# The last half output group of a decoder layer, computed token set by token set, and warm-up matmuls in its first stage

## The chip, the cores and the metric

The kernel runs on one core of one Trainium2 chip. The metric is the device time of one execution in microseconds (us), the median of several runs.

## What is computed

One layer of a decoder over 320 tokens (256 prompt tokens, 8 samples of 8 tokens), width 4096. Attention, indexer and pooling branches end in a mixed activation of 4096 channels. Only this part of the reference bears on the change:

```
h = einsum('btd,dn->btn', rmsnorm(x, ln_g), w_in)       # input projection, 14496 columns
...
mix = concatenate([o_a * silu(g_a), o_b * silu(g_b)])
y = x + einsum('btm,md->btd', mix, w_out)                # w_out 4096 x 4096
rmsnorm(y, g) = y * rsqrt(mean(y*y, axis=-1) + 1e-6) * g # final norm, over all 4096 columns
```

## The kernel before, in words

**Products.** Activations stand in SBUF with channels on the partitions and tokens on the free axis, split into a high and a low part (`XH`, `XL`, type fp32r). Weights come in chunks of 512 rows by 256 columns (`raw`, four slots). ACT rounds a chunk to `hi` (`hi_chunk`, L238), DVE subtracts to get `lo` (`lo_chunk`, L242), and PE forms hi·XH, hi·XL and lo·XH with the weights stationary and all 320 tokens moving (`products`, L267 to L269): 24 matmuls of 320 columns to a chunk. In the segment `qi` a shorter form is used (`paired`, L254 and L255): 512 and 256 moving columns.

**Order.** A group is 512 output columns: two halves of 8 chunks each. Each engine runs its own program over the chunks j = 0..15 of a group (`pe_quad`, `act_quad`, `dve_quad`); extra work is woven in at fixed j. ACT and DVE split chunk j + 3 while PE is at chunk j; a split waits until the chunk four before has been used (`chunk_used`), since `hi` and `lo` have four slots. SP issues the loads, a chunk's load after the `lo` split of the chunk four before it.

**Last stage.** The segment `out` has 8 groups. After a half, DVE copies two banks of 128 channels x 320 tokens to `stg` (L372). PE turns a group's four blocks for the three sets of tokens (128, 128 and 64 tokens; `turn`, L1539, 12 transposes), DVE adds x (`residual`, L1525), ACT squares and sums (`squares`, L1469), POOL multiplies by `final_g` (`weigh`, L1627). For groups 0 to 6 this is woven into the next group. After group 7 nothing follows: copies, turn, residual, squares, the sum (L1669, L1671), the root (L1654), a Newton step (L1679 to L1687), the scaling of all 3 x 4096 columns by DVE (L1688) and ACT (L1655) in eight pieces, and their stores by SP (L1552) and ACT (L1458), 5.2 MB in all.

**First stage.** SP and ACT load the 320 rows of x in five column parts for each of the three sets (`x_part`, L452; parts 0 and 1 are 512 columns, 2 to 4 are 1024), small tensors, and the first chunks (`first_chunk`, 160 columns wide, 320 KB). PE waits for the small tensors, turns them (L595), then for each chunk c turns the next chunk's x (`turn_tokens`, L605: for each of 4 channel blocks two transposes of 128-row sets and one of the 64-row set) and runs `products(c)`. ACT rounds each block to XH (L513), splits weight chunks (L238) and squares x (L524), in that order for each c; DVE makes XL (L542) and `lo`. Chunks 8 and 9, whose splits belong to c = 6, are 256 columns wide.

Of the kernel before, what the change touches and what calls it, by code (L numbers as in the profile page):

```python
# [32 lines left out]
def hybrid_layer(nc, t, out):  # L33
# [90 lines left out]
    with root:  # L124
# [109 lines left out]
        def hi_chunk(act, c, slot, uses, width=2 * P, guard=True):  # L234
# [3 lines left out]
            nc.scalar.activation(hi[:, slot, :, 0:width], raw[:, slot, :, 0:width], ACT.Copy).then_inc(hi_ready, 1)  # L238

        def lo_chunk(dve, c, slot, width=2 * P):  # L240
            dve.wait_ge(hi_ready, c + 1)
            nc.vector.tensor_tensor(lo[:, slot, :, 0:width], raw[:, slot, :, 0:width],  # L242
                                    hi[:, slot, :, 0:width].bitcast(F32), ALU.subtract).then_inc(lo_ready, 1)
# [28 lines left out]
        def pe_quad(pe, name, q, weave=None, before=None, first=False, last=False):  # L272

            _, _, _, c0, quad0, _ = segs[name]
            for j in range(QC):
# [17 lines left out]
        def act_quad(act, name, q, weave=None, last=False, turned=None, gate=None, open_end=False):  # L293

            _, _, _, c0, quad0, tile0 = segs[name]
            for j in range(QC):
                k = j + AHEAD_SPLIT
                half = j // CH
                if not (last and k >= QC):
# [46 lines left out]
        def dve_quad(dve, name, q, weave=None, last=False, turned=None, gate=None, open_end=False, first=False):  # L346
# [3 lines left out]
            for j in range(QC):  # L350
                k = j + AHEAD_SPLIT
                if not (last and k >= QC):
                    lo_chunk(dve, q * QC + (c0 + k), (c0 + k) % SLOTS)
                if j in ends.values():
# [45 lines left out]
        s_onehot, s_wi = sem("s_onehot"), sem("s_wi")  # L400
# [23 lines left out]
        def first_stage(ph):  # L424
# [20 lines left out]
            junk = keep[:, G * N:G * N + XW]  # L445

# [7 lines left out]
            def on_sync(sp):  # L454
                def first_chunk(c):
                    load_chunk(sp, c, c % SLOTS, w_rows["w_in"][:, KK * c:KK * c + KK, C_WI:C_WI + W0], W0, c >= SLOTS)
                sp.dma_start(ident[:], t["c_ident"]).then_inc(s_small, 16)
                x_part(sp, 0, 0)
                sp.dma_start(gN[:], t["ln_g"][0].rearrange("(k p) -> k p", p=P)).then_inc(s_small, 16)
                sp.dma_start(pscN[:], t["pool_scale"][0].rearrange("(k p) -> k p", p=P)).then_inc(s_small, 16)  # L460
# [19 lines left out]
            def on_gpsimd(pool, ahead):  # L480
                pool.dma_start(ptab[:], t["page_table"].rearrange("(o b) p -> o (b p)", o=1)).then_inc(s_outA, 16)
# [20 lines left out]
            def on_scalar(act):  # L502
                for part in range(len(X_CUTS)):
                    x_part(act, 1, part)
                    if part < 3:
                        x_part(act, 2, part)
# [23 lines left out]
            def on_vector(dve):  # L530
                nc.vector.memset(ssq[:], 1.0).then_inc(s_step, 1)
# [61 lines left out]
            def on_tensor(pe):  # L593
                pe.wait_ge(s_small, 48)
# [4 lines left out]
                def turn_tokens(c):  # L599
                    for k in range(KK * c, KK * c + KK):  # L600
# [652 lines left out]
        def last_stage(ph):  # L1253
# [6 lines left out]
            assert DECK >= 3 * D + 8 * P  # L1260
# [21 lines left out]
            y = [deck[:, i * D:(i + 1) * D] for i in range(3)]  # L1282
            gq, sqj = (deck[:, 3 * D + 4 * P * i:3 * D + 4 * P * (i + 1)] for i in range(2))
            NQ_OUT = segs["out"][2]
            sq = sb("sq", [P, 3, NQ_OUT], ctx=ph)
            ms = sb("ms", [P, 3], ctx=ph)
            rt = sb("rt", [P, 3], ctx=ph)
            nt = sb("nt", [P, 3], ctx=ph)
            rf = sb("rf", [P, 3], ctx=ph)
# [89 lines left out]
            def dve_weave(dve, q, j):  # L1379
# [21 lines left out]
                if s == 6:  # L1401
# [6 lines left out]
            (f_mul, f_hi, f_lo, f_t, f_add, f_sq, f_gq, f_g, f_sum, f_rt, f_rf, f_x, f_gd) = (sem(n) for n in (  # L1408
                 "f_mul", "f_hi", "f_lo", "f_t", "f_add", "f_sq", "f_gq", "f_g", "f_sum", "f_rt", "f_rf", "f_x", "f_gd"))
            f_y = {e: sem(f"f_y_{e}") for e in ("act", "dve")}  # L1410
            f_out = {e: sem(f"f_out_{e}") for e in ("act", "dve")}
# [25 lines left out]
            def gate_branch(pool, m):  # L1437
# [8 lines left out]
            CUTS = {"dve": ((0, 0, D // 2), (0, D // 2, D), (2, 0, D // 2), (2, D // 2, D)),  # L1446
                    "act": ((1, 0, D // 4), (1, D // 4, D // 2), (1, D // 2, 3 * D // 4), (1, 3 * D // 4, D))}

            def scaled(eng, name, mul):
                eng.wait_ge(f_rf, 1)  # L1450
                eng.wait_ge(f_g, NQ_OUT)
                eng.wait_ge(f_gd, 1)
                for n, (i, a, z) in enumerate(CUTS[name]):
                    r = TT[i][1]
                    mul(y[i][0:r, a:z], rf[0:r, i:i + 1]).then_inc(f_y[name], 1)
                    if name != "dve":
                        eng.wait_ge(f_y[name], n + 1)
                        eng.dma_start(outs[i][:, a:z], y[i][0:r, a:z]).then_inc(f_out[name], 16)  # L1458
                if name != "dve":
                    eng.wait_ge(f_out[name], 16 * len(CUTS[name]))  # L1460

            def squares(act, q):

                for i in range(3):
# [5 lines left out]
                                         accum_out=sq[0:r, i, ds(q, 1)]).then_inc(f_sq, 1)  # L1470

# [54 lines left out]

            def dve_out_weave(dve, q, j):
                if j == 2:
                    residual(dve, q - 1)

# [16 lines left out]
            def on_sync(sp):  # L1547
                load_segment(sp, "ga")
                load_segment(sp, "out")
                for n, (i, a, z) in enumerate(CUTS["dve"]):  # L1550
                    sp.wait_ge(f_y["dve"], n + 1)
                    sp.dma_start(outs[i][:, a:z], y[i][0:TT[i][1], a:z]).then_inc(f_out["dve"], 16)  # L1552
                sp.wait_ge(f_out["dve"], 16 * len(CUTS["dve"]))

# [14 lines left out]
            def on_gpsimd(pool):  # L1569
# [48 lines left out]
                def weigh(q, tiles_):  # L1618
# [6 lines left out]
                    for i in tiles_:  # L1625
                        cols = y[i][0:TT[i][1], ds(q * (4 * P), 4 * P)]
                        ins = nc.gpsimd.tensor_tensor(cols, cols, gq[0:TT[i][1], :], ALU.mult)  # L1627
                    ins.then_inc(f_g, 1)

                with pool.Fori(0, NQ_OUT - 1) as q:  # L1630
# [3 lines left out]
                    weigh(q, (0, 1, 2))  # L1634
                weigh(NQ_OUT - 1, (0, ))
# [4 lines left out]
            def on_scalar(act):  # L1640
# [10 lines left out]
                act_quad(act, "out", NQ_OUT - 1, act_out_weave, True, turned=f_t)  # L1651
                squares(act, NQ_OUT - 1)
                act.wait_ge(f_sum, 3)
                nc.scalar.activation(rt[:], ms[:], ACT.Sqrt).then_inc(f_rt, 1)  # L1654
                scaled(act, "act", lambda o, r: nc.scalar.activation(o, o, ACT.Copy, scale=r))  # L1655

            def on_vector(dve):
# [8 lines left out]
                dve_quad(dve, "out", NQ_OUT - 1, dve_out_weave, True, turned=f_t)  # L1666
                residual(dve, NQ_OUT - 1)
                dve.wait_ge(f_sq, 3 * NQ_OUT)
                nc.vector.tensor_reduce(ms[:], sq[:], AX.X, ALU.add).then_inc(f_sum, 1)  # L1669
                dve.wait_ge(f_sum, 2)  # L1670
                nc.vector.tensor_scalar(ms[:], ms[:], 1.0 / D, EPS, ALU.mult, ALU.add).then_inc(f_sum, 1)  # L1671
                dve.wait_ge(f_gq, 16 * NQ_OUT)
                for i in (1, 2):
                    cols = y[i][0:TT[i][1], D - 4 * P:D]
                    ins = nc.vector.tensor_tensor(cols, cols, gq[0:TT[i][1], :], ALU.mult)
                ins.then_inc(f_gd, 1)

                dve.wait_ge(f_rt, 1)
                nc.vector.reciprocal(rt[:], rt[:]).then_inc(f_sum, 1)  # L1679
                dve.wait_ge(f_sum, 4)  # L1680
                nc.vector.tensor_tensor(nt[:], rt[:], rt[:], ALU.mult).then_inc(f_sum, 1)
                dve.wait_ge(f_sum, 5)
                nc.vector.tensor_tensor(nt[:], nt[:], ms[:], ALU.mult).then_inc(f_sum, 1)
                dve.wait_ge(f_sum, 6)
                nc.vector.tensor_scalar(nt[:], nt[:], -0.5, 1.5, ALU.mult, ALU.add).then_inc(f_sum, 1)
                dve.wait_ge(f_sum, 7)
# [117 lines left out]
```

## Time and profile before

| | us |
|---|---|
| median of three runs (2142.09 to 2143.4) | 2143.34 |
| the profiled execution | 2144.88 |
| its span, first to last instruction | 2143.4 |
| PE busy in the span | 2099.1 |

The span is what the instructions cover; 1.5 us lie around it. Engines: PE is the matmul engine, PEld its weight loads, DVE the vector engine, ACT the scalar engine, POOL the general engine; SP only issues transfers. A matmul's row shows its whole passage; matmuls overlap, so the distance between starts is what one costs. A name in square brackets after a row is what ended the idle time before it.

### The profile page before, as it was taken

What the parts mean: (1) busy time and instruction counts of PE and PEld (TensorE: products, weight loads), DVE (VectorE), ACT (ScalarE), POOL (GpSimd) and SP (SyncE); (2) the same over time, 40 slices, a digit from 0 to 9 for tenths busy, and PEclk for the clock granted to TensorE, in tenths of its full rate; (3) what the DMA queues carried; (4) which work ended last, traced back from release to release, by engine and by line L of the source; (5) the groups of instructions that cost most, each with busy time, mean ns of one, the idle gap of its engine ahead of it and who ended that gap; (6) DMA issues with size and microseconds to landing.
All of it is one profiled execution on the core that took longest, in us unless ns stands there. A gap on an engine that the chain in (4) does not pass through costs nothing.

```text
span 2143.4 us, 38938 instructions
## 1 busy us (share of the span) xinstructions
PE 2099.1 (98%) x14287; PEld 1996.1 (93%) x14287; DVE 1156.0 (54%) x1375; ACT 741.4 (35%) x911; POOL 404.1 (19%) x560
## 2 busy tenths in 40 slices
PE   7999999999999999999999999999999999999994
PEld 6888888899999999999999999999999999999994
DVE  4545454555555445656776667655656644444442
ACT  5433333332323333333332323333334333333332
POOL 0100000021211010235660102222223211111110
PEclk9999999999999999999999999999999999999998
DMA  6677777755554566566665657777777655555553
GB/s 191 188 222 212 215 213 207 226 155 154 157 154 138 175 186 174 174 197 182 201 184 175 186 166 212 241 233 224 228 229 258 216 165 163 161 160 162 163 152 108
DMA packets 339501, 402.38 MB, mean 188 GB/s; under 512 B 20173, under 2 KB 316301, under 8 KB 338793
## 3 DMA queue, kind: packets, MB, share of 16 engines
q1 hardware_dynamic: 293736, 294.53, 47.0%
q0 software_dynamic: 27952, 86.77, 12.7%
q10 hardware_dynamic: 17744, 20.19, 2.8%
q8 instruction: 41, 0.67, 0.1%
q14 instruction: 28, 0.22, 0.0%
HBM read 374.04 MB, written 31.51 MB: 189 GB/s over the span
## 4 chain that ended last, share of the span: by engine, by line
PE 93%; DMA 2%; POOL 2%; DVE 1%; ACT 1%; issue 0%; SPq 0%; ACTq 0%; POOLq 0%; DVEq 0%
PE bank L267 22%; PE bank L269 22%; PE bank L268 22%; PE bank L254 11%; PE bank L255 6%; PE wide L749 1%; PE wide L1314 1%; PE wide L1159 1%; PE wide L1344 1%; PE wide L1327 1%; POOL ubuf L1044 1%; PE wide L605 1%; PE wide L726 1%; DMA projT<-stg 1%; DMA xN<-x_prompt 1%; PE wide L1539 0%
## 5 line engine op out<-in xcount | busy, mean ns | idle before, releaser
L267 PE MATMUL bank<-XX,hi 128*128 128x320 f32 x3392 | 1072.7, 316 | 2.9 <-DVE XX L1484 2.9
L242 DVE TENSOR_TENSOR lo<-raw,hi 128x1024 fp32r<-128x1024 f32 (+1 forms) x552 | 700.9, 1274 | 667.4 <-ACT hi L238 666.8
L269 PE MATMUL bank<-XX,lo 128*128 128x320 f32 x3392 | 1051.2, 310 | 0.0
L268 PE MATMUL bank<-XX,hi 128*128 128x320 f32 x3392 | 1051.0, 310 | 0.0
L238 ACT ACTIVATE hi<-raw 128x1024 fp32r<-128x1024 f32 (+1 forms) x552 | 577.0, 1052 | 868.6 <-PE bank L269 547.0
L267 PEld LDWEIGHTS bank<-XX,hi 128*128 128x128 f32 x3392 | 639.3, 188 | 12.6 <-issue 5.0
L268 PEld LDWEIGHTS bank<-XX,hi 128*128 128x128 f32 x3392 | 639.5, 189 | 2.1
L269 PEld LDWEIGHTS bank<-XX,lo 128*128 128x128 f32 x3392 | 638.9, 188 | 0.0
L254 PE MATMUL bank<-XX,hi 128*128 128x512 f32 x1024 | 355.7, 392 | 0.0
L255 PE MATMUL bank<-XX,lo 128*128 128x256 f32 x1024 | 287.1, 280 | 0.0
L254 PEld LDWEIGHTS bank<-XX,hi 128*128 128x128 f32 x1024 | 191.6, 187 | 42.0 <-issue 0.2
L255 PEld LDWEIGHTS bank<-XX,lo 128*128 128x128 f32 x1024 | 193.9, 189 | 0.0
L1627 POOL TENSOR_TENSOR deck<-deck 128x512 f32 (+2 forms) x22 | 34.7, 1598 | 368.9 <-ACT deck L1469 368.9
L495 POOL DMA_DIRECT2D biasP<-biasD x16 | 8.7, 541 | 283.9 <-PE bank L255 283.9
L764 ACT ACTIVATE relu<-wide 128x384 f32<-128x384 f32 (+1 forms) x32 | 14.0, 437 | 120.0 <-PE wide L726 86.9
L370 DVE TENSOR_TENSOR stg<-bank,rstdB 128x320 f32<-128x320 f32 x72 | 32.0, 485 | 39.8 <-PE bank L269 39.8
L669 POOL DMA_DIRECT2D ipg<-cache_idx_k x64 | 34.6, 541 | 99.8 <-issue 99.8
L1559 POOL DMA_DIRECT2D deck<-cache_k x64 | 34.5, 540 | 97.1 <-issue 97.1
L1012 POOL DMA_DIRECT2D oT<-ohT x16 | 8.8, 549 | 176.9 <-ACT ohT L1187 176.9
L1227 DVE MAX8 tops<-scS 64x8 f32<-64x1032 f32 x32 | 39.1, 1221 | 0.0
L1044 POOL TENSOR_TENSOR ubuf<-ubuf 128x1816 f32<-128x1816 f32 (+3 forms) x10 | 38.8, 3879 | 0.8
L1559 POOL DMA_DIRECT2D keep<-cache_v x40 | 21.5, 537 | 91.2 <-issue 91.2
(244 smaller groups left out, 1309.3 us busy)
## 6 DMA issues: line engine op xcount, KB each, us to landing
raw<-w_in SPq DMA_DIRECT2D x416, 512.0 KB, 3.8
raw<-w_out SPq DMA_DIRECT2D x128, 512.0 KB, 3.7
deck<-cache_k POOLq DMA_DIRECT2D x64, 256.0 KB, 4.1
projT<-stg ACTq DMA_DIRECT2D x36, 320.0 KB, 2.9
keep<-cache_v POOLq DMA_DIRECT2D x40, 256.0 KB, 3.3
deck<-cache_v POOLq DMA_DIRECT2D x24, 256.0 KB, 3.8
ipg<-cache_idx_k POOLq DMA_DIRECT2D x64, 64.0 KB, 2.6
wp<-w_pool POOLq DMA_DIRECT2D x4, 1024.0 KB, 6.0
```

The costliest lines, as they stand in the source:

```text
L238: nc.scalar.activation(hi[:, slot, :, 0:width], raw[:, slot, :, 0:width], ACT.Copy).then_inc(hi_ready, 1)
L242: nc.vector.tensor_tensor(lo[:, slot, :, 0:width], raw[:, slot, :, 0:width], hi[:, slot, :, 0:width].bitcast(F32), ALU.subtract).then_inc( ...
L254: nc.tensor.matmul(both, wh, XX[:, k, :, FREE:N], start=first, stop=False)
L255: mm = nc.tensor.matmul(bank[banks[n]][:, LATE:2 * LATE], wl, XX[:, k, 0, FREE:N], start=False, stop=last)
L267: nc.tensor.matmul(sums, wh, XH[:, k, :], start=first, stop=False)
L268: nc.tensor.matmul(sums, wh, XL[:, k, :], start=False, stop=False)
L269: mm = nc.tensor.matmul(sums, wl, XH[:, k, :], start=False, stop=last)
L669: pool.dma_start(ipg[:, p, :], tile_rows(t["cache_idx_k"][0], page)).then_inc(s_ipg, 16)
L1044: done(nc.gpsimd.tensor_tensor(dst[:, :, lost + w:UW], src[:, :, lost + w:UW], src[:, :, lost:UW - w], ALU.add))
L1227: nc.vector.max(tops[:], scS[:]).then_inc(ts_step, 1)
L1559: pool.dma_start(dst[p], tile_rows(src, page)).then_inc(landed, 16)
L1627: ins = nc.gpsimd.tensor_tensor(cols, cols, gq[0:TT[i][1], :], ALU.mult)
```

## The change

The last group's second half is computed with the tokens stationary and 256 weight columns moving. Its first half is turned and added on its own, after chunk 1 of the second half. Chunks 0 and 1 are multiplied for all three sets; then chunks 2 to 7 for set 0, then for set 1, then for set 2. Chunks 6 and 7 get buffers of their own (`late`), so that no weight is overwritten. After each set's products: residual, squares, root, Newton step, scaling in seven pieces and six stores for this set alone. The last 256 columns of `final_g` are multiplied in by DVE with the scaling. The output rows move to buffers that outlive the stage (`ends`, and `keep` for set 2).

In the first stage PE starts with 16 bf16 matmuls of 512 columns on zeros. SP's order of loads changes, x parts 3 and 4 go to POOL's queue behind the landing of part 0, and `turn_tokens` turns the eight 128-row blocks first and then the four 64-row blocks.

```diff
+            def set_products(pe, i, m):
+                c0, r = TT[i]
+                for kk in range(KK):
+                    k = (KK * m + kk + KT // 2) % KT
+                    wh, wl = (w[:, kk, :] for w in weights[m])
+                    sums = bank[SETS[i]][0:r, 0:HB]
+                    nc.tensor.matmul(sums, XH[:, k, c0:c0 + r], wh, start=m == 0 and kk == 0, stop=False)
+                    nc.tensor.matmul(sums, XL[:, k, c0:c0 + r], wh, start=False, stop=False)
+                    mm = nc.tensor.matmul(sums, XH[:, k, c0:c0 + r], wl, start=False, stop=m == CH - 1 and kk == KK - 1)
+                return mm
+            def pe_last_half(pe):
+                pe.wait_ge(evac[1], Z + (quad0 + 1))
+                for m in range(CH):
+                    pe.wait_ge(lo_ready, c + 1)
+                    for i in range(3 if m < NOW else 1):
...
+                        mm = set_products(pe, i, m)
+                    mm.then_inc(chunk_used if m < CH - 1 else f_prod, 1)
+                    if m == 1:
+                        last_turn(pe)
+                for i in (1, 2):
+                    for m in range(NOW, CH):
+                        mm = set_products(pe, i, m)
+                    mm.then_inc(f_prod, 1)
+            def act_end_weave(act, q, j):
+                act_out_weave(act, q, j)
+                if j == 10:
+                    for i in range(3):
+                        half_square(act, i, 0, 3 * Z + i)
+                if j == 12:
+                    nc.scalar.activation(rt[:], sq[:, :, 0], ACT.Sqrt).then_inc(f_rt, 1)
...
             def on_scalar(act):
...
+                act.wait_ge(f_g, NQ_OUT)
+                for i in range(3):
+                    half_square(act, i, 1, 3 * NQ_OUT + i)
+                    last_root(act, i)
+                    act_scaled(act, i)
...
             def on_vector(dve):
...
+                for i in range(3):
+                    dve.wait_ge(f_prod, i + 1)
+                    last_residual(dve, 1, i)
+                    last_norm(dve, i)
+                    dve_scaled(dve, i)
...
             def on_sync(sp):
+                sp.dma_start(gN[:], ...)
+                sp.dma_start(pscN[:], ...)
                 sp.dma_start(ident[:], t["c_ident"]).then_inc(s_small, 16)
                 x_part(sp, 0, 0)
-                sp.dma_start(gN[:], ...)
-                sp.dma_start(pscN[:], ...)
+                x_part(sp, 0, 1)
                 first_chunk(0)
-                x_part(sp, 0, 1)
                 x_part(sp, 0, 2)
-                first_chunk(1)
-                first_chunk(2)
-                x_part(sp, 0, 3)
-                x_part(sp, 2, 3)
-                first_chunk(3)
-                x_part(sp, 0, 4)
-                x_part(sp, 2, 4)
+                for c in range(1, SLOTS):
+                    first_chunk(c)
...
             def on_gpsimd(pool, ahead):
+                pool.wait_ge(s_x[0], 48)
+                for part in (3, 4):
+                    for i in range(3):
+                        x_part(pool, i, part)
...
             def on_tensor(pe):
+                pe.wait_ge(s_zeros, 1)
+                for _ in range(WARM):
+                    nc.tensor.matmul(bank[1][:, 0:512], zeros[:, 0:P], zeros, start=True, stop=True)
                 pe.wait_ge(s_small, 48)
...
-                        for i, (c0, r) in enumerate(TT):
-                            tr = nc.tensor.transpose(sbank[k % 4][:, c0:c0 + r], xN[i][0:r, k * P:k * P + P],
-                                                     ident[0:r, 0:r])
-                        tr.then_inc(s_xT, 1)
+                        for i, (c0, r) in enumerate(TT[0:2]):
+                            nc.tensor.transpose(sbank[k % 4][:, c0:c0 + r], xN[i][0:r, k * P:k * P + P], ident[0:r, 0:r])
+                    for k in range(KK * c, KK * c + KK):
+                        nc.tensor.transpose(sbank[k % 4][:, T_P:N], xN[2][0:N_S, k * P:k * P + P],
+                                            ident[0:N_S, 0:N_S]).then_inc(s_xT, 1)
```

## Rows read from the trace of the kernel before

**Rows 1.** The page of the profile: busy time by engine, and the chain by engine.

```profile
PE 2099.1 (98%) x14287; PEld 1996.1 (93%) x14287; DVE 1156.0 (54%) x1375; ACT 741.4 (35%) x911; POOL 404.1 (19%) x560
...
PE 93%; DMA 2%; POOL 2%; DVE 1%; ACT 1%; issue 0%; SPq 0%; ACTq 0%; POOLq 0%; DVEq 0%
```

**Rows 2.** The view of waits, for PE: who waited for whom, us in total, times, longest.

```profile
PE bank L595 <- DMA pscN<-pool_scale: 7.7, 1, 7.7
```

**Rows 3.** The timeline of the end: start us, us, engine, line, operation, tiles, shapes.

```profile
2115.05 0.89 DVE L372 COPY stg<-bank 128x320 f32<-128x320 f32 x2 [11.70 <-PE bank L269]
...
2116.03 1.50 PE L1539 MATMUL wide<-ident,stg 128*128 128x128 f32 x12 [1.03 <-issue]
2117.64 1.88 DVE L1525 TENSOR_TENSOR deck<-wide,deck 128x512 f32<-128x512 f32 x3 [1.71 <-PE wide L1539]
2118.42 0.63 ACT L1469 ACTIVATE deck<-deck 128x512 f32<-128x512 f32 x1 [16.33 <-DVE deck L1525]
2118.95 0.19 ACT L1469 ACTIVATION_READ_ACCUMULATOR deck<-deck 128x1 f32 x1
...
2123.37 0.16 DVE L1679 RECIPROCAL rt<-rt 128x3 f32<-128x3 f32 x1
...
2124.16 0.16 DVE L1687 TENSOR_TENSOR rf<-rt,nt 128x3 f32<-128x3 f32 x1
2124.36 1.15 ACT L1655 ACTIVATE deck<-deck,rf 128x1024 f32<-128x1024 f32 x1 [1.86 <-DVE rf L1687]
2124.36 4.87 DVE L1688 TENSOR_SCALAR deck<-deck,rf 128x2048 f32<-128x2048 f32 x4
...
2130.31 0.35 ACTq L1458 DMA_DIRECT2D out<-deck  x1
```

**Rows 4.** The DMA view from 2100 us to the end: rate in 40 equal slices.

```profile
GB/s 0 0 0 0 0 0 0 0 0 0 0 0 0 0 0 15 0 0 0 0 0 0 0 0 417 391 458 402 402 421 369 253 242 250 264 253 238 376 30 0
```

**Rows 5.** Windows of the end, PE alone: window, us, PE busy, granted clock, DMA share, GB/s.

```profile
2120.00:2124.00 4.00, 0.00 (x0) 0.86 0.00 0
```

**Rows 6.** The timeline around 68 us, PE: matmuls that move 256 and 512 columns.

```profile
68.10 0.28 PE L255 MATMUL bank<-XX,lo 128*128 128x256 f32 x1
68.10 0.19 PEld L254 LDWEIGHTS bank<-XX,hi 128*128 128x128 f32 x1
68.22 0.40 PE L254 MATMUL bank<-XX,hi 128*128 128x512 f32 x1
...
68.45 0.28 PE L255 MATMUL bank<-XX,lo 128*128 128x256 f32 x1
```

**Rows 7.** The timeline of the last half group: one split on ACT, one on DVE.

```profile
2093.99 1.06 ACT L238 ACTIVATE hi<-raw 128x1024 fp32r<-128x1024 f32 x1 [2.46 <-PE bank L269]
...
2098.60 1.23 DVE L242 TENSOR_TENSOR lo<-raw,hi 128x1024 fp32r<-128x1024 f32 x1 [2.29 <-ACT hi L238]
```

**Rows 8.** The timeline of the first stage, PE and ACT.

```profile
14.16 0.74 ACT L238 ACTIVATE hi<-raw 128x640 fp32r<-128x640 f32 x1 [1.88 <-DMA raw<-w_in]
...
16.09 3.73 PE L605 MATMUL wide<-ident,xN 128*128 128x128 f32 x12 [4.37 <-DMA xN<-x_prompt]
...
19.75 0.63 PE L267 MATMUL bank<-XX,hi 128*128 128x320 f32 x1
...
25.13 2.30 PE L605 MATMUL wide<-ident,xN 128*128 128x128 f32 x12
...
42.07 1.06 ACT L524 ACTIVATE keep<-xN 128x1024 f32<-128x1024 f32 x1
...
43.27 2.24 ACT L513 ACTIVATE XX<-wide,gT 128x320 fp32r<-128x320 f32 x4
...
60.37 0.42 PE L267 MATMUL bank<-XX,hi 128*128 128x320 f32 x1
```

**Rows 9.** The DMA view of the first stage, issues from 3.1 to 3.4 us: KB, us to landing.

```profile
raw<-w_in SPq DMA_DIRECT2D x1, 320.0 KB, 11.2
xN<-x_prompt SPq DMA_DIRECT2D x1, 256.0 KB, 12.7
```

More of the change, by code:

```diff
@@ L270, in products, with pe_quad @@
             mm.then_inc(chunk_used, 1)
-        def pe_quad(pe, name, q, weave=None, before=None, first=False, last=False):
+        def pe_quad(pe, name, q, weave=None, before=None, first=False, last=False, stop=QC):
             _, _, _, c0, quad0, _ = segs[name]
-            for j in range(QC):
+            for j in range(stop):
                 half, pos, rot = chunk_at(name, j, first, last)
@@ L344, in act_segment, with dve_quad @@
                 act_quad(act, name, q, weave, gate=gate)
-        def dve_quad(dve, name, q, weave=None, last=False, turned=None, gate=None, open_end=False, first=False):
+        def dve_quad(dve, name, q, weave=None, last=False, turned=None, gate=None, open_end=False, first=False, homes=None):
             _, _, _, c0, quad0, _ = segs[name]
@@ L351, in dve_quad @@
                 k = j + AHEAD_SPLIT
-                if not (last and k >= QC):
+                if homes and k in homes:
+                    lo_chunk(dve, q * QC + (c0 + k), k % SLOTS, homes=homes[k])
+                elif not (last and k >= QC):
                     lo_chunk(dve, q * QC + (c0 + k), (c0 + k) % SLOTS)
-                if j in ends.values():
+                if j in ends.values() and not (homes and j == QC - 1):
                     half = chunk_at(name, j, first)[0]
@@ L502, in on_scalar @@
             def on_scalar(act):
-                for part in range(len(X_CUTS)):
+                for part in range(3):
                     x_part(act, 1, part)
-                    if part < 3:
-                        x_part(act, 2, part)
+                    x_part(act, 2, part)
                 act.wait_ge(s_step, 1)
@@ L1443, in gate_branch @@
                 ins.then_inc(f_mul, 1)
[L1446 to L1460, printed above, removed]
+            Z = NQ_OUT - 1
@@ new lines, in last_stage @@
+            HB = 2 * P
+            Z = NQ_OUT - 1
+            HB = 2 * P
+            homes = {QC - 2 + n: (late[:, 2 * n, :, :], late[:, 2 * n + 1, :, :]) for n in range(2)}
+            weights = [homes.get(CH + m, (hi[:, m % SLOTS, :, :], lo[:, m % SLOTS, :, :])) for m in range(CH)]
+            NOW = 2
+            assert segs["out"][3] % SLOTS == 0 and CH == 2 * SLOTS
+            SETS = (2, 3, 0)
+            CUTS = {"dve": ((0, D // 8), (D - HB, D), (D // 8, 5 * D // 16), (5 * D // 16, D // 2)),
+                    "act": ((D // 2, 5 * D // 8), (5 * D // 8, 13 * D // 16), (13 * D // 16, D - HB))}
@@ L1525, in residual, with last_residual, last_turn @@
                     nc.vector.tensor_tensor(cols, sbank[i][0:r, :], cols, ALU.add).then_inc(f_add, 1)
+            def last_residual(dve, half, i):
+                r = TT[i][1]
+                cols = y[i][0:r, half_cols(half)]
+                turned = bank[SETS[i]][0:r, 0:HB] if half else sbank[i][0:r, 0:HB]
+                nc.vector.tensor_tensor(cols, turned, cols, ALU.add).then_inc(f_add, 1)
+            def last_turn(pe):
+                pe.wait_ge(evac[0], segs["out"][4] + Z + 1)
+                pe.wait_ge(f_add, 3 * Z)
+                for i, (c0, r) in enumerate(TT):
+                    for n in range(2):
+                        tr = nc.tensor.transpose(sbank[i][0:r, n * P:(n + 1) * P], stg[0][:, n, c0:c0 + r], ident[:])
+                tr.then_inc(f_t, 1)
             def dve_out_weave(dve, q, j):
@@ L1650, in on_scalar @@
                     act_quad(act, "out", q, act_out_weave, turned=f_t)
[L1651 to L1655, printed above, removed]
+                act_quad(act, "out", Z, act_end_weave, True, turned=f_t, homes=homes)
+                act.wait_ge(f_g, NQ_OUT)
+                for i in range(3):
+                    half_square(act, i, 1, 3 * NQ_OUT + i)
+                    last_root(act, i)
+                    act_scaled(act, i)
             def on_vector(dve):
@@ L1711, in hybrid_layer @@
             prompt = prompt_stage(place)
-        last = last_stage(root)
+        last = last_stage()
         stages = (first, index, topk, prompt, last)
```

169 lines of the change are left out of this document (115 added, 54 removed).

## Prediction, made before the changed kernel was run

> **What bounds the kernel now.** I read the page first. PE is busy 98% of the span and carries 93% of the chain that ended last [rows 1]. So an edit pays only where PE idles or where its work shortens. PE idles in two places of any size: at the start, until the small tensors have landed at 7.7 us [rows 2] and again 4.37 us for x at 16.09 [rows 8]; and at the end, where the last product is through at 2115.0 and the span runs to 2143.4. The change works on exactly these two places.
>
> **The end before** [rows 3]. From 2115.0 on one step follows another: two copies 0.89, twelve transposes 1.50, three residual adds 1.88, three squares (0.63 + 0.19 each), the root, reciprocal and Newton steps to 2124.3, scaling to 2130.3, and the stores. The stores are the largest part: data moves from 2126.4, first at about 400, then at about 250 GB/s [rows 4], to the end. That is 28.4 us behind PE.
>
> **Part 1, the products of the last half.** A chunk on PE takes 2.46 + 1.06 = 3.52 us, the distance between two splits that each wait for PE [rows 7]; with 24 matmuls that is 0.1467 us for 320 columns, 0.458 ns a column. The last half (8 chunks, 192 matmuls) therefore costs 28.2 us and starts at 2086.8. The new form has 3 sets x 32 blocks x 3 = 288 matmuls of 256 columns. A 256-column matmul starts at 68.10, the next at 68.22, and 768 columns take 0.35 us from 68.10 to 68.45 [rows 6]: 0.46 ns a column again, with a 128-column weight load inside each. I take 256 x 0.458 = 0.1173 us: 288 of them are 33.8 us, **5.6 us more** on PE. Set 2 has half the tokens and pays the same, since the weights move. The page "TensorE: Matmul & The Clock Gate" of the Trainium skill, in "Back-to-back issue gap", gives columns / 2.4 + 2.5 ns; that would be 109 ns for 256 columns and 2.4 us less in all, but it also gives 136 ns for 320 columns, where the trace has 147, so the trace decides.
>
> **Inside the last half.** Chunks 0 and 1 take 36 matmuls each, 8.4 us, to 2095.2. Six transposes of the first half, at half of 1.50 us, reach 2096.0. Chunk 4 of the half is split once chunk 0 has been used, and is in time. The split of chunk 5 waits for chunk 1 (2095.2): ACT to 2096.3, DVE to 2097.6. Then DVE adds the first half for three sets, 0.38 each (a 512-column add takes 0.63, a 320-column copy 0.45 [rows 3]), and ACT squares them, about 0.63 each, to 2099.9. Only behind these squares in ACT's queue stand the splits of chunks 6 and 7 (1.06 each on ACT, 1.23 on DVE [rows 7]): ready at 2102.3 and 2103.5. PE takes 12 matmuls, 1.41 us, for a chunk of set 0 and would want chunk 6 at 2101.6. So it stalls about 0.7 us, and set 0 is through at 2105.1. Loads don't matter: the last one is issued under the split of chunk 3, near 2089, while PE wants it after 2102. POOL's last multiply waits for the squares and ends near 2102.5. The square-root table is fetched behind the last split, under set 0's products. Sets 1 and 2 need 72 matmuls each: 2113.5 and **2122.0**.
>
> **Each set's tail.** From the last product: residual 0.15 + 0.38, square and sum 0.7, root 0.25, reciprocal and three steps at 0.20 each [rows 3], so about 2.4 us to the scale factor. ACT's three pieces (1792 columns at 1.15 per 1024, plus three issues of 0.35 to 0.4 and gaps) take 3.4 us; DVE's take 1.8 and run beside. Set 0: last store issued at 2111. Set 1: at 2119.4. Its 2.1 MB at 250 GB/s, the slower rate of [rows 4], would be through at 2125 even from 2116.5. Set 2: scale factor at 2124.4, last store issued at 2127.6. It moves only 1.05 MB, 4.2 us at 250 GB/s from 2125.7. Both ways lead to 2130 to 2130.5. The span ends at 2130.5 instead of 2143.4: **12.9 us less**. What hides the cost of sets 0 and 1 is set 2's own products, 8.4 us a set against a tail of 5.8 us of engines and 8.4 us of stores at the slower rate.
>
> Bounds: at 0.109 a matmul, the distance of the transposes, (1.50 - 0.3) / 11 [rows 3], the gain is 15.3; if the two sets' stores drag into the third's, or splits stall PE 3 us more, 9.9.
>
> **Part 2, the first stage.** Before, products(0) starts at 19.75 [rows 8]. x part 1 of set 0 lands at 3.4 + 12.7 = 16.1, behind chunk 0 of the weights (2.9 + 11.2 = 14.1) in SP's queue [rows 9]. The change puts it ahead, so PE turns chunk 1's x near 10 us. Then products(0) waits for chunk 0. That transfer now has 256 KB more ahead of it on SP and POOL's 2.5 MB beside it from about 8 us, and 1 MB less on ACT's queue beside it. It can land at 12 to 17; I take 13.5, near the 14.1 of before. Rounding 0.74, DVE's subtraction 0.83 and gaps make it ready at 15.2: 4.5 us earlier than before.
>
> The warm-up matmuls aim at the clock. The trace shows half rate at the start: 12 transposes at 16.09 take 3.73, at 25.13 they take 2.30; products(0) takes 5.38 us from 19.75 to 25.13 where a chunk normally takes 3.52. So the lower level costs 1.9 us there (1.2 against 2.4 GHz). But after the warm-ups PE has only transposes until 15.2, with pauses for loads. At the end of the old trace the granted clock averages 0.86 over 2120 to 2124 although nothing ran there after 2117.5 [rows 5]: it falls a few microseconds after PE stops. I take it as lost again, and products(0) as slow as before, to 20.6. The Trainium skill's page "TensorE: Matmul & The Clock Gate", "Part 1: The HAM clock gate", says the same: the half rate is the default, and idling brings it back.
>
> From there ACT sets the pace, not PE. PE's cycle shortens: the 64-row transposes stand in one run instead of four, and twelve transposes with one change of shape should take about 1.4 in place of 2.13 us (2.30 with the overlap [rows 8]; twelve without such changes take 1.50 with it [rows 3]). A cycle would be 4.9 instead of 5.7. But ACT's work for a chunk is 2.24 for XH, 0.74 or 1.36 for splits and 2 x 1.25 for squares (1.06, and 0.19 for the sum as in [rows 3]) [rows 8]: 5.5, 5.5, 6.1, 6.1 and, with the two wide splits, 6.9 us for c = 2 to 6, together 30.0. With x of chunk 2 turned from 20.6 on, ACT starts on it at 21.4 and on chunk 7 at 51.4; DVE follows to 53.9; products(7) ends at 57.4. Before it started at 60.37 and ended 63.9 [rows 8]. **6.5 us less.** PE is the bound behind it, so the shift is carried to the end. Bounds: chunk 0 at 17 gives 3; at 12, with the clock kept, 9. Below that, loads held up further by POOL's queue could take all of it.
>
> What else moves: POOL's six issues stand before its page-table load, whose first user is far later; the wait for part 0 holds nothing else. ACT issues two transfers fewer. The memset for the warm-ups puts 0.3 us before DVE's others, hidden by the 7 us of loads. Longer straight-line code for PE I cost at nothing: the fetch runs beside the matmuls, and group 0 is straight-line too. If fetching failed, PE would pay it fully.
>
> **Sum.** 12.9 + 6.5 = 19.4 us. The profiled execution took 2144.88, of which 1.5 lie around the span: 2125.5. The median stands 1.5 below that execution: **2123.9**. A measurement tells about 0.2% (4.3 us) from no change.
>
> **Rivals.**
> *The first stage keeps its length* (chance 0.20). Speaking for it: three queues now draw on the same DMA engines, 320 KB took 11.2 us there with two, and ACT is nearly full. Against: what PE waited for at 16.09 was one transfer's place in a queue. Gain 1.5 there: 2143.3 - 12.9 - 1.5 = 2128.9.
> *The end gives less* (0.10). ACT and DVE serve the splits, squares and tails in one order each; each late split stalls PE. With 4 us lost: 2127.9.
> *Stationary loads are exposed* (0.03), the slower side. If a load of tokens were not hidden under 256 moving columns, a matmul would cost 0.117 + 0.109 = 0.226 (the load priced as a transpose, which has one of the same size under it), and the 288 would be 65.1 us: 31.3 more, 2155.2. It decides from (19.4 / 288) + 0.117 = 0.185 us a matmul. Against it stand [rows 6], a load under each of two neighbouring matmuls. For it: there the short ones come only every second time.
> *The warm-ups hold the clock* (0.15, inside the forecast): 1 us less, since ACT then binds: 2122.9.
>
> **How the numbers follow.** My forecast holds 0.67 with the last rival in it: 2120 to 2127.5. The range goes to the other two faster cases and the bounds: 2118 to 2131. Slower by over 0.2% is the exposed load, 0.03; within 0.2% needs both parts to fail by 15 us together, 0.03; faster 0.94.
>
> **What would show it.** Starts of the new matmuls 0.117 apart; the last one near 2115.5 on the new clock (2122.0 less 6.5); three stores of PE-covered sets; 8.4 us from PE's last product to the end; products(0) starting near 15 at 0.27 a matmul; products(7) starting near 53.9 behind DVE. I am wrong if the matmuls stand over 0.13 apart, if PE waits for splits over 2 us, or if products(7) starts after 58.

## The result, and the profile after

The changed kernel takes **2126.2 us** (2123.5 to 2127.8, four runs) against 2142.7 (2140.6 to 2143.4, four runs) of the kernel before, run beside it: ratio 0.9922, 95% interval 0.9910 to 0.9934, 16.5 us less. The forecast was 2123.9, within 2118 to 2131, and 19.4 us less. The profiled execution took 2127.56, its span is 2126.0, 17.4 us less than before. The page, as [rows 1]; the span's chain is followed back only to the last set's root here, so it has nothing to compare:

```profile
PE 2101.1 (99%) x14385; PEld 2001.3 (94%) x14393; DVE 1157.3 (54%) x1393; ACT 743.1 (35%) x925; POOL 406.7 (19%) x568
```

To see where the gain lies I cut every span at two instants: where DVE sums the squares of the first stage (L547 before, L554 after), and where DVE makes the last two copies of 128x320 (L372, L378), with which the last half begins.

| | first stage, to the sum of squares | middle | end, from the last copies |
|---|---|---|---|
| before | 62.66 | 2024.2 | 56.5 |
| after | 58.03 | 2022.1 | 45.8 |
| difference | -4.6 | -2.1 | -10.7 |

The first cut lies behind ACT and DVE. What is passed on to the middle is PE's part, the start of products(7): 60.37 before [rows 8], 56.63 now, 3.7 us earlier. Counted from there the middle is 3.0 us shorter, though the change does not touch it.

**The end.** The three sets on DVE, each from its residual add, and the last set's steps (the timeline of the changed kernel, DVE):

```profile
2099.35 0.43 DVE L1598 TENSOR_TENSOR ends<-bank,ends 128x256 f32<-128x256 f32 x1 [1.58 <-PE bank L1641]
...
2107.81 0.42 DVE L1598 TENSOR_TENSOR ends<-bank,ends 128x256 f32<-128x256 f32 x1 [4.17 <-PE bank L1641]
...
2116.05 0.42 DVE L1598 TENSOR_TENSOR keep<-bank,keep 64x256 f32<-64x256 f32 x1 [4.02 <-PE bank L1641]
...
2117.42 0.16 DVE L1530 RECIPROCAL rt<-rt 128x1 f32<-128x1 f32 x1 [0.16 <-ACT rt L1520]
...
2118.13 0.16 DVE L1537 TENSOR_TENSOR rf<-rt,nt 128x1 f32<-128x1 f32 x1
2118.32 0.48 DVE L1482 TENSOR_SCALAR keep<-keep,rf 64x512 f32<-64x512 f32 x1
```

The same on ACT, set 2:

```profile
2116.50 0.42 ACT L1513 ACTIVATE ends<-keep 64x256 f32<-64x256 f32 x1 [3.18 <-DVE keep L1598]
...
2118.32 0.72 ACT L1489 ACTIVATE keep<-keep,rf 64x512 f32<-64x512 f32 x1 [0.94 <-DVE rf L1537]
...
2121.95 0.49 ACTq L1494 DMA_DIRECT2D out<-keep  x1
```

The adds stand 8.46 and 8.24 us apart: one set's products each. The last one starts at 2116.05; its scale factor is ready 2.3 us later, ACT's last store is issued at 2121.95, and the span ends at 2126.0, 9.95 us behind the last add. PE's last product ends at 2116.0, so the span runs on for 10.0 us behind PE, where it was 28.4. Now PE, in the same timeline:

```profile
2096.20 0.28 PE L1641 MATMUL bank<-late,XX 128*128 128x256 f32 x1
2096.32 0.28 PE L1639 MATMUL bank<-late,XX 128*128 128x256 f32 x1
2096.44 0.28 PE L1640 MATMUL bank<-late,XX 128*128 128x256 f32 x1
...
2115.73 0.28 PE L1641 MATMUL bank<-late,XX 128*64 128x256 f32 x1
```

A 256-column matmul with a fresh 128-column load costs 0.12 us, start to start; on set 2, whose load has 64 columns, it costs 0.115. The DMA view in two windows, from 2109 to 2117.5 and from 2117.5 to 2126 (40 slices of 0.21 us each):

```profile
GB/s 0 0 0 0 0 0 0 0 0 0 0 164 366 424 337 405 376 424 376 419 376 376 419 390 376 419 405 376 376 419 376 376 420 419 419 361 275 0 0 0
```

```profile
GB/s 0 0 0 0 0 0 0 0 0 0 0 0 241 183 183 260 183 202 241 202 231 231 217 217 202 159 188 188 217 231 231 232 217 202 159 116 0 0 0 0
...
out<-keep SPq DMA_DIRECT2D x2, 192.0 KB, 3.2
out<-keep ACTq DMA_DIRECT2D x2, 192.0 KB, 3.8
```

Set 1's 2.1 MB move at 380 to 420 GB/s, under set 2's products. Set 2's 1.05 MB move at 210 (four pieces of 192 KB and two of 128) and take 5.0 us, from 2120.05 to 2125.1.

**The first stage.** ACT's rows (chunk 0, chunk 1, XH of chunk 2, XH of chunk 7), then PE's:

```profile
15.32 0.74 ACT L239 ACTIVATE hi<-raw 128x640 fp32r<-128x640 f32 x1 [1.76 <-DMA raw<-w_in]
...
23.84 0.74 ACT L239 ACTIVATE hi<-raw 128x640 fp32r<-128x640 f32 x1 [6.12 <-DMA raw<-w_in]
...
25.53 1.76 ACT L519 ACTIVATE XX<-wide,gT 128x320 fp32r<-128x320 f32 x4
...
54.10 1.76 ACT L519 ACTIVATE XX<-wide,gT 128x320 fp32r<-128x320 f32 x4
```

```profile
1.48 5.98 PE L603 MATMUL bank<-keep 128*128 128x512 bf16 x16 [1.48 <-DVE keep L537]
...
17.06 0.60 PE L268 MATMUL bank<-XX,hi 128*128 128x320 f32 x1 [1.30 <-DVE lo L244]
17.46 0.47 PE L269 MATMUL bank<-XX,hi 128*128 128x320 f32 x1
...
21.95 1.04 PE L615 MATMUL wide<-ident,xN 128*128 128x128 f32 x8
22.91 0.46 PE L617 MATMUL wide<-ident,xN 64*128 64x64 f32 x4
25.59 0.38 PE L268 MATMUL bank<-XX,hi 128*128 128x320 f32 x1 [2.21 <-DVE lo L244]
...
27.40 0.47 PE L269 MATMUL bank<-XX,hi 128*128 128x320 f32 x1
27.66 0.47 PE L270 MATMUL bank<-XX,lo 128*128 128x320 f32 x1
...
30.71 1.04 PE L615 MATMUL wide<-ident,xN 128*128 128x128 f32 x8
...
35.68 1.03 PE L615 MATMUL wide<-ident,xN 128*128 128x128 f32 x8
...
56.63 0.41 PE L268 MATMUL bank<-XX,hi 128*128 128x320 f32 x1 [0.92 <-DVE XX L549]
```

The warm-ups run from 1.48 to 7.4. Chunk 0 is split at 15.32, products(0) start at 17.06, 2.7 us earlier than in [rows 8], and at 0.27 us each until 19.9. Then comes a wait that did not exist before: chunk 1 is split only at 23.84, when it has landed, so products(1) start at 25.59; and from 26.9 to 30.1 the matmuls stand 0.27 apart once more. From 30.71 to 50.58 PE's five turns start 4.97 us apart, and PE does not wait until it is held up for 0.92 us before products(7). The granted clock of these stretches (windows of PE alone, the number behind the count in brackets):

```profile
2.00:7.00 5.00, 5.00 (x15) 1.00 0.77 226
7.00:12.00 5.00, 3.15 (x17) 0.77 1.05 252
12.00:17.00 5.00, 2.65 (x12) 0.50 1.06 309
17.00:22.00 5.00, 4.94 (x25) 0.71 1.05 338
22.00:27.00 5.00, 2.79 (x22) 0.98 1.09 259
27.00:32.00 5.00, 5.00 (x29) 0.68 0.66 174
```

It is 0.50 (1.2 GHz) from 12 to 17, and goes down twice: before the first products, and again after the pause for chunk 1 (0.68 on average from 27 to 32). The 1.00 from 2 to 7 can't be taken at its word: the 16 warm-ups last 5.98 us, where matmuls of the same kind cost about 0.215 us each at full rate (six in 1.47, four in 1.04, in e6 below), so most of them ran at the lower level. The column also reads 1.00 in the kernel before while its first products stand 0.27 apart [rows 8]. Before its first change the distance between starts is the measure, not this column. PE's waits of the changed kernel:

```profile
PE bank L268 <- DVE lo L244: 3.5, 2, 2.2
PE wide L1177 <- DMA uin<-projT: 2.5, 1, 2.5
PE wide L615 <- DMA xN<-x_prompt: 1.8, 1, 1.8
...
PE bank L1639 <- DVE late L244: 0.8, 1, 0.8
```

### The profile page after: what moved, and what is told of

Read it like the earlier page. It is cut to its first block and busy times, and to the rows that moved or that the text cites. A ratio compares the mean times of both kernels' runs of the same rounds, so it can differ in the third digit from the quotient of the medians.

```text
span 2126.0 us, 39179 instructions
## 1 busy us (share of the span) xinstructions
PE 2101.1 (99%) x14385; PEld 2001.3 (94%) x14393; DVE 1157.3 (54%) x1393; ACT 743.1 (35%) x925; POOL 406.7 (19%) x568
## 5 line engine op out<-in xcount | busy, mean ns | idle before, releaser
L268 PE MATMUL bank<-XX,hi 128*128 128x320 f32 x3328 | 1051.7, 316 | 5.8 <-DVE lo L244 3.5
L270 PE MATMUL bank<-XX,lo 128*128 128x320 f32 x3328 | 1030.3, 310 | 0.0
L269 PE MATMUL bank<-XX,hi 128*128 128x320 f32 x3328 | 1030.0, 309 | 0.0
L268 PEld LDWEIGHTS bank<-XX,hi 128*128 128x128 f32 x3328 | 626.9, 188 | 15.6 <-issue 8.8
L269 PEld LDWEIGHTS bank<-XX,hi 128*128 128x128 f32 x3328 | 627.0, 188 | 2.1
L270 PEld LDWEIGHTS bank<-XX,lo 128*128 128x128 f32 x3328 | 626.5, 188 | 0.0
L255 PEld LDWEIGHTS bank<-XX,hi 128*128 128x128 f32 x1024 | 191.5, 187 | 42.3 <-issue 0.2
L256 PEld LDWEIGHTS bank<-XX,lo 128*128 128x128 f32 x1024 | 193.5, 189 | 0.0
L1761 POOL TENSOR_TENSOR ends<-ends 128x512 f32 (+1 forms) x16 | 26.1, 1650 | 346.1 <-ACT ends L1503 328.7
L1240 DVE MATCH_REPLACE8 scS<-tops,scS 64x1032 f32<-64x1032 f32 x32 | 38.6, 1208 | 0.0
```

The lines of the kernel that those rows point to most:

```text
L255: nc.tensor.matmul(both, wh, XX[:, k, :, FREE:N], start=first, stop=False)
L256: mm = nc.tensor.matmul(bank[banks[n]][:, LATE:2 * LATE], wl, XX[:, k, 0, FREE:N], start=False, stop=last)
L268: nc.tensor.matmul(sums, wh, XH[:, k, :], start=first, stop=False)
L269: nc.tensor.matmul(sums, wh, XL[:, k, :], start=False, stop=False)
L270: mm = nc.tensor.matmul(sums, wl, XH[:, k, :], start=False, stop=last)
L1240: nc.vector.match_replace(scS[:], tops[:], scS[:], TAKEN).then_inc(ts_step, 1)
```

## The experiments

Times are medians with the kernel before run beside each; the columns "first stage", "middle" and "end" are cut from each run's profile at the instants above.

| kernel | median us | ratio to before (95%) | first stage | middle | end |
|---|---|---|---|---|---|
| changed kernel | 2126.2 | 0.9922 (0.9910 to 0.9934) | 58.03 | 2022.1 | 45.8 |
| e1 head only | 2136.1 | 0.9968 (0.9956 to 0.9979) | 55.74 | 2022.7 | 56.5 |
| e2 tail only | 2130.8 | 0.9933 (0.9920 to 0.9946) | 62.64 | 2022.0 | 45.95 |
| e3 no warm-ups | 2126.7 | 0.9920 (0.9907 to 0.9933) | 55.76 | 2023.6 | 45.9 |
| e4 old turn | 2128.6 | 0.9927 (0.9915 to 0.9939) | 60.16 | 2018.3 | 45.9 |
| e5 x later | 2124.7 | 0.9913 (0.9898 to 0.9928) | 53.58 | 2023.4 | 45.85 |
| e6 x later, clock held | 2121.9 | 0.9898 (0.9883 to 0.9913) | 52.31 | 2021.6 | 46.0 |
| e7 together | 2133.2 | 0.9953 (0.9937 to 0.9969) | 55.24 | 2020.1 | 55.8 |
| e8 rebalanced | 2123.3 | 0.9914 (0.9897 to 0.9931) | 54.30 | 2020.1 | 45.9 |
| e9 three chunks for all | 2122.9 | 0.9908 (0.9891 to 0.9924) | 55.80 | 2020.7 | 44.55 |
| e10 e6 + e9 | 2122.3 | 0.9902 (0.9885 to 0.9918) | 52.61 | 2025.7 | 44.6 |
| e11 e10 + part 2 later | 2120.3 | 0.9892 (0.9875 to 0.9908) | 51.96 | 2024.1 | 44.6 |
| e12 long rows (one run) | 2129.95 | | 55.24 | 2025.8 | 47.3 |

The end repeats within 0.15 us over the six kernels that share its code (the changed one and e2 to e6), the middle varies by 7.6 us in code that none of these edits touches. So an edit of the end is read from its column, not from the median; the first stage needs several profiles.

**e1 and e2, one half of the change each.** e1 is the kernel before with the new first stage, e2 the changed kernel with the old one.

> The kernel before with the new first stage alone, its end unchanged. Theory (two separate gains that add): the last half group starts 6.7 us earlier, as in the changed kernel (2080.1 against 2086.8), and the median is 6.7 us below that of the kernel before (ratio 0.9969). Rival (the first stage keeps its length and the whole gain is from the end): within 2 us of the kernel before. The first products start near 17.1 us at 0.27 us each.

> The changed kernel with the first stage of before. Theory: the end alone gives 10.7 us (the stretch from the start of the last half to the end of the span is 45.9 us instead of 56.6), ratio 0.995. Rival (the earlier end needs the new first stage, or part of the gain is common to both): under 8 us.

Measured: e1 has 6.9 us less in the first stage and an unchanged end, ratio 0.9968; e2 has an unchanged first stage and 10.6 us less at the end, ratio 0.9933. The two gains are separate and add up: by the cuts 6.9 + 10.6 = 17.5 us, where the span of the changed kernel is 17.4 shorter; by the medians 0.9968 x 0.9933 = 0.9901, a little below the changed kernel's interval. (e2's median is 13.6 us below the kernel before, 3 more than its end gives; its profile has the middle 2.2 us shorter.) The rival that the first stage keeps its length falls.

**e3, no warm-ups.**

```diff
-            WARM = 16
+            WARM = 0
```

> The changed kernel without its 16 warm-up matmuls. Theory (the clock falls back before the first products, so they buy nothing): time of the changed kernel within 0.7 us, first products again at 0.27 us each for the first 3 us or so. Rival (they shorten the stretch at half rate): 1 to 3 us slower than the changed kernel, more than 11 products at 0.27.

The first products start at 16.60, 0.5 us earlier, at the lower clock again; the medians are 0.5 us apart, and each interval is over 5 us wide, so a gain of 1 us would not show in them. The distance of 0.27 lasts longer than expected: it stands 20 times in products(0), against 9 in the changed kernel's profile. That is the rival's sign, but the warm-ups don't explain it: five more profiles with the same warm-ups and the same loads (e1, e7, e8, e9, e12) have it 20, 16, 4, 14 and 15 times. Their first stages are 54.3 to 55.8 us long, e3's is 55.76. So the warm-ups buy between nothing and 1.5 us where they stand, and these runs can't tell which.

**e4, the old order of the transposes,** in the changed kernel.

```diff
-                        for i, (c0, r) in enumerate(TT[0:2]):
+                        for i, (c0, r) in enumerate(TT):
...
-                    for k in range(KK * c, KK * c + KK):
-                        nc.tensor.transpose(sbank[k % 4][:, T_P:N], ...
```

> The changed kernel with the transposes of the first stage in their old order (three sets for each block). Theory (PE's turn takes 2.13 instead of 1.4 us and ACT gets the blocks one by one): cycles of 5.8 us instead of 5.0 for chunks 2 to 6, the last half starts 2.5 to 4 us later than in the changed kernel. Rival (ACT sets the pace anyway): under 1 us later, with ACT without idle time between 30 and 54 us.

The first stage ends at 60.16, against 54.3 to 55.8 in the six experiments with the new order and the same loads (e1, e3, e7, e8, e9, e12; 58.03 in the changed kernel's own profile). So the new order of the transposes is worth 4 to 6 us against these (2.1 against the changed kernel's own profile, which lost time at chunk 1), more than half of the first stage's gain. PE's rows show it free of that scatter: in e4 PE turns from 22.62 on every 5.84 us and never waits, in the changed kernel every 4.97, as expected (5.8 and 5.0): 0.87 us for each chunk. In ACT's rows of e4 XH of a chunk takes 2.24 us where ACT follows the turn block by block, and 1.77 for the last chunk, whose blocks had all been turned before ACT came; in the changed kernel every chunk from the second on takes about 1.76:

```profile
34.93 2.24 ACT L519 ACTIVATE XX<-wide,gT 128x320 fp32r<-128x320 f32 x4 [0.67 <-PE wide L615]
...
55.35 1.77 ACT L519 ACTIVATE XX<-wide,gT 128x320 fp32r<-128x320 f32 x4
```

The rival, that ACT sets the pace anyway, falls.

The median of e4 is 2.4 us above the changed kernel's, but the ratios overlap: this profile has the shortest middle of all (2018.3), and that hides the loss in its span (its last half starts 1.75 us earlier than the changed kernel's, not 2.5 to 4 later as expected).

**e5 and e6, what feeds the first products.**

```diff
-                pool.wait_ge(s_x[0], 48)
+                pool.wait_ge(s_x[2], 48)
```

> The changed kernel, but POOL issues x parts 3 and 4 when part 2 has landed (near 17 us) and not when part 0 has (9.5 us). Theory (POOL's 2.5 MB beside SP's queue make chunk 0 land at 15.3 and chunk 1 at 23.8): chunk 0 lands 1 to 2 us and chunk 1 3 to 5 us earlier, PE no longer waits 2.2 us for the split of chunk 1, 2 to 3 us faster than the changed kernel. Rival (the queue of SP alone, with its short rows, sets these landings): no change, and x parts 3 or 4 may come late, near 30 us or later.

Chunk 1 is split at 17.17 instead of 23.84, chunk 0 at 14.49 instead of 15.32; PE's wait for splits falls from 3.5 to 0.4 us, and PE now waits longer for x:

```profile
PE wide L615 <- DMA xN<-x_prompt: 4.3, 2, 2.2
...
PE bank L268 <- DVE lo L244: 0.4, 1, 0.4
```

The first stage ends at 53.58, about 2 us earlier than in e1, e3, e9. The theory holds for chunk 1: in the eight profiles with POOL's early issue it is split at 21.1 to 23.8, in the four with the later one (e5, e6, e10, e11) at 16.4 to 17.3. So POOL's 2.5 MB had been in its way. For chunk 0 it is not shown: without the edit it is split at 14.3 to 15.3, and 14.49 lies among these. The median is 1.5 us below the changed kernel's where 2 to 3 were expected, and the intervals overlap. e6 adds three groups of matmuls on zeros:

```diff
+                fill(6)
                 turn_tokens(0)
+                fill(4)
...
+                    if c == 0:
+                        fill(6)
```

> As the run before it, with 6, 4 and 6 more matmuls on zeros: behind the first 16, between the first two turns, and ahead of the first products. Theory (the clock is kept only by work close to the products): the first products stand 0.147 apart from the start, 1.3 to 1.9 us less for chunk 0; the added matmuls cost up to 1.5 us where loads were already in, so 0 to 1.5 us faster than the run before it. Rival (the clock falls anyway because the transposes in between do not keep it): first products at 0.27, 0 to 2 us slower.

The last fill runs until 15.6; the first products stand 0.147 apart from the second on (timeline of e6, PE):

```profile
14.15 1.47 PE L604 MATMUL bank<-keep 128*128 128x512 bf16 x6
16.43 0.39 PE L268 MATMUL bank<-XX,hi 128*128 128x320 f32 x1 [0.82 <-DVE lo L244]
16.66 0.31 PE L269 MATMUL bank<-XX,hi 128*128 128x320 f32 x1
16.81 0.31 PE L270 MATMUL bank<-XX,lo 128*128 128x320 f32 x1
```

Products(0) take 3.6 us instead of 5.1, and the first stage ends 1.3 us earlier than in e5 (one profile each; the ratios overlap). So the clock can be held: with fills in all three pauses, the last ending 0.8 us before the first product, no product stands 0.27 apart, while in every profile with warm-ups at the start alone some do. Which of the three fills is needed was not tried.

**e7, the three sets together.** All chunks for all sets, then three tails in a row; the same 288 matmuls.

```diff
-            NOW = 2
+            NOW = CH
...
-                for i in (1, 2):
-                    for m in range(NOW, CH):
-                        mm = set_products(pe, i, m)
-                    mm.then_inc(f_prod, 1)
```

> The changed kernel, but all three sets take every chunk, so that all sets end together and none of their adds, roots, scalings and stores lies under products. The same 288 matmuls. Theory (what pays is the stagger): PE ends up to 0.8 us earlier (no wait for the splits), then three tails of 5.9 us in a row and stores behind: 12 us slower than the changed kernel, near the kernel before. Rival (the shorter pieces and the first half done early are what pays): under 5 us slower.

The end is 55.8 us: 10 us longer than with the stagger (12 expected) and 0.7 shorter than before; the median is 7.0 us above the changed kernel's. The rival, under 5 us, falls. So what is left of the change without the stagger (smaller pieces, the first half finished early) just pays for the 5.6 us of extra products; the stagger is the gain. The stores then begin late and all stand behind PE (DMA view, 2100 to 2131):

```profile
GB/s 0 0 0 0 0 0 0 0 0 0 0 0 0 0 0 0 0 114 391 394 389 400 389 404 284 378 407 381 396 408 389 289 122 211 211 226 202 194 186 0
```

**e8, DVE scales 2560 columns of a set, ACT 1536 in two pieces.**

```diff
-            CUTS = {"dve": (..., (5 * D // 16, D // 2)),
-                    "act": ((D // 2, 5 * D // 8), (5 * D // 8, 13 * D // 16), (13 * D // 16, D - HB))}
+            CUTS = {"dve": (..., (5 * D // 16, 9 * D // 16)),
+                    "act": ((9 * D // 16, 3 * D // 4), (3 * D // 4, D - HB))}
```

> The changed kernel with DVE scaling 2560 columns of each set and ACT 1536 in two pieces (before: 2304 and 1792 in three). Theory (ACT's queue, 0.72 + 0.94 + 0.72 us of scaling and three issues, ends last): the last store is issued 1.1 us earlier and the span ends about 1 us earlier. Rival (the stores of 64 rows at 210 GB/s end last, whoever issues them): under 0.4 us.

```profile
2110.73 0.42 ACT L1513 ACTIVATE ends<-keep 64x256 f32<-64x256 f32 x1 [4.11 <-DVE keep L1598]
...
2115.09 0.50 ACTq L1494 DMA_DIRECT2D out<-keep  x1
```

From the square to ACT's last issue it is now 4.4 us where it was 5.45 (2116.50 to 2121.95), and the end is 45.9: nothing gained. The rival was right: the stores of 64 rows end last, not the engine that issues them (their data moves from about 2114.3 to 2119.4, at 210 GB/s again). Its lower median comes from a short first stage and middle.

**e9, three chunks for all sets.**

```diff
-            NOW = 2
+            NOW = 3
```

> The changed kernel with three chunks, not two, multiplied for all sets before set 0 runs ahead. Theory (PE waits 0.85 us for the splits of chunks 6 and 7, which one more chunk of 4.2 us covers; a stagger of 7.0 us still covers a tail of 5.9): the stretch from the last copies to the end of the span falls from 45.9 by 0.8 to 1.1 us. Rival (the shorter stagger lets the stores or tails of two sets meet): not shorter than 45.7.

The end is 44.55, 1.3 us less, a little more than the 0.85 that PE waited for the first of the two late splits; in the changed kernel there was a second, shorter hitch between the last two chunks of set 0 (0.26 us between two starts at 2097.5). In e9 PE does not wait for a split in the last half.

**e10 and e11, the gains put together.** e10 joins e6 and e9. e11 lets ACT issue x part 2 when part 0 has landed.

> x parts 3 and 4 later, the clock held up to the first products, and three chunks for all sets. Theory (the gains of e6 and e9 add): first stage as in e6 (its sum over squares near 52.3 us), last stretch as in e9, a median 1 us below that of e6, 5 us below the changed kernel.

> As e10, and ACT issues its two transfers of x part 2 when part 0 has landed. Theory (what is not needed yet takes the DMA engines from chunk 0 and x part 1): chunk 0 lands 1 to 2 us earlier, first products near 15, the first stage ends 0 to 1.5 us earlier than in e10. Rival (part 2 then becomes what the second chunk waits for, or the engines were not full): no gain, PE waits for x before its third turn.

First stage and end are as expected (52.6 and 44.6), but e10's median is 0.4 us above that of e6, where 1 below was expected: its profile has a middle of 2025.7, 4.1 us longer than that of e6. e11's first products start at 15.97 instead of 16.73 and its first stage ends 0.65 us earlier than e10's. At 2120.3 us, ratio 0.9892, e11 has the lowest median of all; against e6 and e10 the intervals overlap, against the changed kernel they don't.

**e12, long rows.** Set 2 stored in two transfers of 512 KB.

> The changed kernel, but set 2 is stored in two transfers of rows of 8 KB when all its columns of a half are scaled, not in six of 1 to 3 KB. Theory (64 rows are slow by their number, not their length: 250 GB/s with 8 KB rows before, 210 now): rate 210 to 250, the stores start 2 us later, last stretch 0.5 to 2 us longer. Rival (short rows cost the rate): 350 GB/s or more and a last stretch no longer than 45.9.

```profile
GB/s 367 426 377 426 386 198 0 0 0 0 0 0 0 0 0 0 0 0 0 0 211 211 291 132 291 132 185 238 79 344 79 344 79 344 26 396 0 0 0 0
...
out<-keep SPq DMA_DIRECT2D x1, 512.0 KB, 4.3
out<-keep ACTq DMA_DIRECT2D x1, 512.0 KB, 6.3
```

Set 2 moves in 4.9 us, 214 GB/s, and the end is 1.5 us longer. Rows of 8 KB are no faster than rows of 1 to 3 KB; and set 1, stored in the same pieces by the same two queues but with 128 rows, moved at 380 to 420. So the rate of these stores goes with the 64 rows, not with the length of a row.

## Why the prediction was right, and where it was off

- **PE idles only at the two ends.** Right: e1 and e2 separate them and they add up.
- **The matmul of 256 columns, 0.1173 us.** Right: 0.12 start to start, a set of 72 takes 8.24 to 8.46 (8.44 forecast). The rival of exposed loads is gone. The 109 ns by the Trainium skill's page "TensorE: Matmul & The Clock Gate", "Back-to-back issue gap", would have made a set 7.9.
- **The stall of 0.7 us at chunk 6.** Right in place and size: 0.85. It was the term that e9 removed. DVE's two late splits took 3.38 us together instead of 2 x 1.23. Why is open: POOL multiplied beside them, but by its rows only until 2096.4, and the second split was as slow as the first; the splits also write to another buffer, and no run parts the two:

```profile
2080.16 0.89 DVE L378 COPY stg<-bank 128x320 f32<-128x320 f32 x2 [1.14 <-PE bank L270]
...
2094.10 3.38 DVE L244 TENSOR_TENSOR late<-raw,late 128x1024 fp32r<-128x1024 f32 x2 [2.08 <-ACT late L239]
```

- **"Through at 2122.0", 35.2 us after the last half begins.** Measured 35.85, 0.65 more. The stall and the second hitch are 0.3 of it; the rest was not taken apart.
- **"Both ways lead to 2130 to 2130.5", 8.5 us behind PE: this step failed.** It was 10.0. The mechanism, stores of the last set, was right, its size was not: I took 250 GB/s from a mixed stretch of [rows 4], and 64-row stores run at 210, which is 5.0 us instead of 4.2; data starts about 0.35 us later than forecast, and 0.9 us pass from the last slice with data to the end of the span. I also held ACT's chain and the stores to be equal bounds; e8 shows that only the stores bind. Together: 12.9 us forecast, 10.7 measured.
- **Products(0) at 15.2.** Late by 1.9: chunk 0 was split at 15.32, inside the range of 12 to 17 but not at the 13.5 taken.
- **The clock.** Right that the warm-ups would be lost before the first products: the granted clock is 0.50 from 12 to 17 us. The Trainium skill's page "TensorE: Matmul & The Clock Gate", "Part 1: The HAM clock gate", says that idling brings the half rate back; the trace agrees. It also came back a second time, once PE had waited 2.2 us for chunk 1. Of the profiles with the early issue only this one shows the second fall; in the others PE waited 1.4 us or less there.
- **"From there ACT sets the pace, not PE": this step failed.** Forecast were 30.0 us of ACT's work from XH of chunk 2 to XH of chunk 7. Measured are 28.6, and 2.75 of them are waits for PE (1.75, 0.74 and 0.26 before three of its rows), so ACT's own work was 25.8: XH takes 1.76 instead of 2.24 when all blocks are there. PE set the pace, with its turns 4.97 us apart (4.9 forecast for its cycle); ACT and DVE held it up only before products(7), for 0.92 us. On the other side I missed chunk 1, at 23.8, and the second fall of the clock: XH of chunk 2 starts at 25.5, not 21.4. So products(7) start at 56.63 instead of 53.9, 3.7 us earlier than before instead of 6.5. In e1, e7, e8, e9 and e12, with the same first stage, they start at 52.9 to 54.4, which is 6.0 to 7.5 us earlier: there the number is met, but by PE's cycle and not by ACT's.
- **"PE is the bound behind it, so the shift is carried to the end".** Not shown: the middle varies by more than the shift. In the profiled pair it gave 3.0 us, counted from products(7), that were not forecast. Without this luck the two parts, 3.7 and 10.7, would have made 14.4 of the forecast 19.4.

## What to carry to other kernels

A last normalisation that needs whole rows holds the stores behind all products. Making the tokens stationary for the last slice, even with 20% more PE time in it, lets the scaling and storing of two sets of three go under products, provided that a set's products last longer than a set's tail; the size of the last set's store is what remains. Warm-up matmuls far ahead of the first real product showed no gain here, fills in the pauses up to it shortened the first stage by 1.3 us in one profile; before adding any, one should ask which load the first product waits for. In a kernel whose middle scatters by several us, cut the profile at fixed instants and judge an edit of an end by its own stretch.

## What had not been expected

The middle is 2018.3 to 2025.8 us long in fourteen profiles. In nine of them PE waits there for one load, `uin<-projT`: 0.9 us in e4 (the shortest middle), 1.9 in e6, 2.5 before and after, 5.2 in e12 (the longest), and in e10

```profile
PE wide L1183 <- DMA uin<-projT: 4.9, 1, 4.9
```

In the other five (e2, e3, e7, e8, e9) PE waits at about that place for DVE instead (`lg`), 1.8 to 2.5 us. Added to PE's waits for DVE's XX further on in the middle (1.4 to 3.3 us) this makes 2.4 us in e4, 3.3 to 3.9 in e6, e7, e8, e9 and the changed kernel (2020.1 to 2022.1), and 6.8 to 6.9 in e10 and e12: the middle goes with it, but varies more than it does. What makes the load late was not tried. The other surprise is the turn: grouped, eight transposes of 128 rows and four of 64 take 1.35 us up to the first product instead of 2.23 (1.4 and 2.13 forecast), and there are six such turns between products.
